# Rotary rotation in a two-layer diffusion backbone: TensorE products replaced by VectorE stream shuffles

## The reference

```python
def apply_rope(x, cos, sin):
    q = HEAD_DIM // 4
    x0, x1, x2, x3 = x[..., :q], x[..., q:2 * q], x[..., 2 * q:3 * q], x[..., 3 * q:]
    rot = jnp.concatenate([-x1, x0, -x3, x2], axis=-1)
    return x * cos + rot * sin
```

## Time and profile before

| what | us |
|---|---|
| median of 3 runs | 1592.22 |
| lowest, highest | 1591.72, 1592.33 |
| the profiled execution | 1592.69 |
| its span in the trace | 1590.7 |

### The profile page before, as it was taken

The page is one execution under the profiler, slowest core; times in us unless marked ns, Lnnn a source line. Parts: engine busy times, 40 slices in busy tenths (PEclk is TensorE's granted clock), DMA queues, the critical chain, the costliest instruction groups (busy, mean ns, idle before and its releaser), DMA issues.

```text
span 1590.7 us, 25340 instructions
## 1 busy us (share of the span) xinstructions
PE 1555.2 (98%) x10789; PEld 1291.7 (81%) x10789; DVE 785.2 (49%) x1276; ACT 550.2 (35%) x725; POOL 538.9 (34%) x243
## 2 busy tenths in 40 slices
PE   7999999899999999999999999999999999999998
PEld 3888764478888888888888888855479998998997
DVE  5898777677466633433234343666533221321224
ACT  5744335563322112221122243255544322322233
POOL 0040046313233233232323223356643444444442
PEclk9999999999999999999999999999999999999999
DMA  9532100052333333334333222200022222223223
GB/s 377 209 119 67 54 28 1 3 215 91 117 110 132 133 111 128 133 119 146 133 128 112 66 80 67 67 14 1 1 68 92 94 93 93 93 94 106 94 93 106
DMA packets 44607, 158.55 MB, mean 100 GB/s; under 512 B 4784, under 2 KB 8240, under 8 KB 42960
## 3 DMA queue, kind: packets, MB, share of 16 engines
q1 hardware_dynamic: 44064, 156.74, 28.5%
q0 software_dynamic: 432, 0.20, 0.1%
HBM read 154.95 MB, written 2.10 MB: 99 GB/s over the span
## 4 chain that ended last, share of the span: by engine, by line
PE 87%; DVE 3%; issue 1%; POOL 1%; ACT 0%; DVEq 0%; POOLq 0%
PE psum L1851 71%; PE psum L2100 3%; PE psum L2068 1%; PE psum L1999 1%; PE psum L1896 1%; PE psum L1928 1%; DVE osb L1381 1%; PE psum L2074 1%; PE psum L2072 1%; PE psum L2070 1%; PE psum L2116 1%; DVE mx L1277 1%; PE psum L1971 1%; POOL acc L622 1%; PE psum L2024 1%
## 5 line engine op out<-in xcount | busy, mean ns | idle before, releaser
L1851 PE MATMUL psum<-act,whi 128*128 128x258 f32 (+2 forms) x3968 | 784.5, 318 | 0.0
L649 POOL TENSOR_TENSOR wlo<-raw,whi 128x1024 fp32r<-128x1024 f32 (+1 forms) x162 | 391.1, 2414 | 792.1 <-ACT whi L683 792.1
L1851 PEld LDWEIGHTS psum<-act,whi 128*128 128x128 f32 x3968 | 587.8, 189 | 57.6 <-issue 3.8
L1851 PE MATMUL psum<-act,wlo 128*128 128x512 f32 (+1 forms) x1984 | 472.1, 316 | 0.0
L1851 PEld LDWEIGHTS psum<-act,wlo 128*128 128x128 f32 x1984 | 309.0, 189 | 26.8
L683 ACT ACTIVATE whi<-raw 128x1024 fp32r<-128x1024 f32 (+1 forms) x180 | 187.1, 1040 | 337.8 <-DMA raw<-weights_dram 337.8
L1178 DVE SCALAR_TENSOR_TENSOR tmps<-psum,rs 128x256 f32<-128x256 f32 (+1 forms) x176 | 78.1, 485 | 350.5 <-PE psum L1851 346.9
L1130 DVE SCALAR_TENSOR_TENSOR product<-adr,cb 128x1024 f32<-128x1024 f32 x128 | 177.5, 1418 | 6.2 <-DMA adr<-adat_dram 3.1
L1620 DVE SCALAR_TENSOR_TENSOR xT<-psum,mod,xT 128x512 f32<-128x512 f32 x93 | 58.3, 655 | 224.4 <-PE psum L1851 224.3
L1851 PE MATMUL psum<-gh,wlo 128*128 128x512 f32 x507 | 152.5, 358 | 0.0
L1851 PE MATMUL psum<-gh,whi 128*128 128x512 f32 x507 | 152.5, 357 | 0.0
(11 more groups left out here) (205 smaller groups left out, 1313.5 us busy)
## 6 DMA issues: line engine op xcount, KB each, us to landing
raw<-weights_dram SPq DMA_DIRECT2D x180, 512.0 KB, 3.5
adr<-adat_dram SPq DMA_DIRECT2D x80, 512.0 KB, 4.7
ada_w<-ada_dram SPq DMA_DIRECT2D x8, 1024.0 KB, 12.5
xT<-x_in_dram SPq DMA_DIRECT2D x3, 1024.0 KB, 16.8
xT<-x_in_dram SPq DMA_DIRECT2D x2, 1536.0 KB, 8.1
cb<-crow_dram SPq DMA_DIRECT2D x2, 1024.0 KB, 9.3
out_dram<-fin SPq DMA_DIRECT2D x8, 256.0 KB, 2.3
stage<-weights_dram SPq DMA_DIRECT2D x1, 512.0 KB, 8.1
```

The lines of the kernel that those rows point to most:

```text
L649: nc.gpsimd.tensor_tensor(wlo[:, s, 0:w], raw[:, s, 0:w], whi[:, s, 0:w].bitcast(F32), ALU.subtract).then_inc(sem("s_lo"), 1)
L1851: last = MM(out_[:, o:o + t1 - t0], w_, a_[:, t0:t1], start=k == order[0] and j == 0, stop=k == order[-1] and j == 2)
```

## The change

`rotated` is gone, with its 14 calls, the permutation matrix in the constants (128 columns) and the waits that kept its PSUM region apart from others. In its place VectorE runs a stream shuffle over the tile, ahead of the sine product: within each group of 32 partitions the halves are swapped (`SWAP`). The signs move into the table of the sine. In layer 0 the shuffle writes `ropet` in SBUF and the sine product works in place; in layer 1 it writes the PSUM bank that the product wrote. VectorE's other work and all orders stay.

```diff
 CC_BLK = CC_ONES + P
-CC_ROT = CC_BLK + P
-CC_MF = CC_ROT + P
+CC_MF = CC_BLK + P
...
+SWAP = [*range(16, 32), *range(16)]
...
         def rot_out(L, j):
 
-            if L == 1:
-                return bank(4 + j % 2)
-            return wk[(j + 1) % 2][:, 0:NX]
+            return bank(4 + j % 2) if L == 1 else ropet[0][:, 0, 0:NX]
...
             def roped_sine(L, j):
+                if L == 0:
+                    dve.wait_ge(sem("a_nrm"), j + 1)
+                    if j >= 1:
+                        dve.wait_ge(sem("a_rope"), j)
+                else:
+                    dve.wait_ge(sem("s_tile"), 19 + (j + 2 if j else 1))
+                V.stream_shuffle(rot_out(L, j), prep_tiles(L)[j][0][:, 0:NX], SWAP).then_inc(sem("a_rot"), 1)
                 dve.wait_ge(*na("rot", L, j + 1))
-                if L == 0 and j >= 1:
-                    dve.wait_ge(sem("a_rope"), j)
                 TT(ropet[L][:, j % 2 * L, 0:NX], rot_out(L, j), sin, ALU.mult).then_inc(sem("a_rsin"), 1)
...
-            def rotated(L, j):
-                if L == 0:
-                    pe.wait_ge(sem("a_nrm"), j + 1)
-                elif j >= 2:
-                    pe.wait_ge(*na("rsin", L, j - 1))
-                MM(rot_out(L, j), rot, prep_tiles(L)[j][0][:, 0:NX], start=True, stop=True) \
-                    .then_inc(sem("a_rot"), 1)
-
...
                 if n == 12:
                     pe.wait_ge(sem("g_kcpD"), 1)
                     means(1)
-                    pe.wait_ge(sem("a_rsin"), 1)
                     linear_keys(2)
                 if n == 13:
                     pe.wait_ge(sem("a_rs"), 2)
-                    rotated(0, 1)
...
                 if n == 14:
                     pe.wait_ge(sem("g_ud"), 2)
                     updates(1)
                     pe.wait_ge(sem("a_rs"), 3)
-                    rotated(0, 2)
...
-                    for m in ready_tiles(b["m"]):
-                        pe.wait_ge(sem("s_tile"), 19 + m + 1)
-                        if m == 1:
-                            values_turned(1)
-                        else:
-                            rotated(1, max(m - 1, 0))
+                    if b["m"] == 2:
+                        pe.wait_ge(sem("s_tile"), 19 + 2)
+                        values_turned(1)
...
-    con[:, CC_SIN:CC_SIN + NX] = np.tile(np.sin(ang), (2, 1))
+    con[:, CC_SIN:CC_SIN + NX] = np.tile(np.sin(ang), (2, 1)) * np.where(np.arange(P) % (2 * quarter) < quarter, -1.0, 1.0)[:, None]
```

More of the change, by code:

```diff
@@ L344, in build @@
         blk = con[:, CC_BLK:CC_BLK + P]
-        rot = con[:, CC_ROT:CC_ROT + P]
         cos = con[:, CC_COS:CC_COS + NX]
@@ L2221, in behind_block @@
                     pe.wait_ge(sem("g_kcpA"), 1)
-                    rotated(0, 0)
                 if n == 12:
@@ L2240, in behind_block @@
                     means(3)
-                    pe.wait_ge(sem("a_rsin"), 3)
                 if n == 16:
                     pe.wait_ge(sem("a_rs"), 4)
-                    rotated(0, 3)
                     pe.wait_ge(*na("mx", 0, 2))
@@ L2250, in behind_block @@
                     rows(0, 0)
-                    rotated(0, 4)
                 if pieces_within(n, 8):
@@ L2266, in within_block @@
                 if n == 14:
-                    pe.wait_ge(sem("a_rsin"), 2)
                     updates(0)
@@ L2271, in within_block @@
                     updates(2)
-                if n == 17:
-                    pe.wait_ge(sem("a_rsin"), 4)
             def gla(sums):
@@ L2394, in _shape_constants @@
     con[:, CC_BLK:CC_BLK + P] = np.kron(np.eye(2), np.ones((64, 64))) / 64.0
[L2395 to L2401, removed]
     j, i = np.arange(CH)[:, None], np.arange(CH)[None, :]
```

## The result

The changed kernel takes 1599.08 us (median of 4 runs, 1597.24 to 1601.56) beside 1591.97 for the kernel before on the same chip (4 runs). The ratio is 1.0044, interval [1.0031, 1.0056]: slower by 0.44%, 7.1 us. The profiled execution took 1600.68 us, with a span of 1597.9. Direction and range held; the size did not: 3.6 us were forecast.

What follows compares the result with a forecast made beforehand. TensorE, busy 98% of the span, was taken as the bound, with VectorE's chain pacing some blocks. Layer 0 +0.86, layer 1 +2.88 and constants -0.1 made +3.6 us, median 1592.22 to 1595.8; range 1592.0 to 1600.5.

Steps and rivals of the forecast that it cites:

- Forecast +0.86: Layer 0's five rotations together: -1.72 + 0.48 + 2.1 = +0.86 us.
- 1.72 - 0.48 = 1.24: Layer 0: first two rotations gain 1.72 us; the third makes TensorE's state updates 0.48 us later.
- 2.1: Layer 0, fourth and fifth rotations: GpSimd's weight split goes ahead of VectorE's scan, making the piece 2.1 us late.
- The rival in which GpSimd does not get in first: Layer 0: the split stays behind the scan, giving -0.4 for +0.86, total +2.4, 1594.6 us; chance 0.27.
- -1.72 was forecast: Layer 1's first two rotations, before the maxima begin: VectorE idle over 3 us, so 1.72 us gained.
- 0.68 + 0.78 + 0.68 + 1.0 = 3.14: Layer 1: delays in blocks 7, 8 and 9, then about +1.0 us at the second score step.
- s: Time from a shuffle's start to its sine product's start: 0.83 us, ends 0.61 and 1.34.
- The rival of the slow shuffle: All shuffles: the shuffle is slow, at the scan's rate; 1600.9 us; chance 0.10.
- the one in which TensorE keeps what it is given: Both layers: all fourteen removed products gained, 12 us, 1580.2 us; chance 0.09, whole or half.
- The further meeting with GpSimd: Layer 0's block 17 or layer 1's last two sums: GpSimd's turn costs another 1.3 to 2.4 us, about 1598; chance 0.14.
- Layer 1: -1.72 + 3.60 + 1.0 = +2.88 us: Layer 1's nine rotations: first two gain 1.72, blocks 5 to 9 lose 3.60, the last two triples lose about 1.0.
- 10 x 0.06: Ten shuffles counted on the path, three in layer 0 and seven in layer 1; each 0.1 us in s makes 1.0 us.

Runs made afterwards that it cites:

- e1_layer0_only: Changed kernel with shuffles in layer 0 only, layer 1's rotations again TensorE products (unsigned permutation, signed sine table); 1592.60 us, 1.0005 of the kernel before.
- e4_filler: Changed kernel with layer 1's shuffle writing SBUF, plus seven unread f32 TensorE products in layer 1; 1594.80 us, 1.0018 of the kernel before.
- e7_layer1_all: e5_reduce_first with layer 1's shuffle writing SBUF and the last two triples behind the last reduction and row tops; 1593.42 us, 1.0013 of the kernel before.
- e9_first_two: Kernel before with shuffles for the first two rotations of each layer, the other ten TensorE products (unsigned permutation, signed table); 1588.55 us, 0.9982.
- e2_layer1_only: Changed kernel with shuffles in layer 1 only, layer 0 as in the kernel before; 1598.21 us, 1.0039 of the kernel before.
- e5_reduce_first: Changed kernel with layer 1's rotary triples, from block 5 on, moved behind the next block's first reduction; 1591.46 us, 1.0001 of the kernel before.
- e11_double: Changed kernel with every shuffle done twice; 1613.87 us, 1.0143 of the kernel before.
- its control: Changed kernel with layer 1's shuffle writing SBUF, all waits kept and no added products; 1601.10 us, 1.0057 of the kernel before.

## Why the prediction was right in direction and short in size

**Layer 0, right at a constant clock.** Forecast +0.86. `e1_layer0_only`, `e4_filler` and `e7_layer1_all` have the same layer 0 and keep a granted clock of 1.00 there; counted from the products at 126 us, their piece of block 18 comes 0.74, 0.71 and 0.73 us late. By the medians, layer 0 alone costs +0.4 (-0.6 to +2.1). Each of its steps is in the trace: the updates behind the third triple wait (1.22 us at 177.16), GpSimd goes ahead of the scan, `statr` gives back a microsecond, block 18's piece is released by VectorE. In `e4_filler` the updates come 1.29 us early by the same count, where 1.72 - 0.48 = 1.24 were forecast, and from there to the piece 2.00 us are lost, where 2.1 were. The rival in which GpSimd does not get in first fell.

In the changed kernel's own profile the clock falls in layer 0 as well (0.83 between 200 and 210 us), and it costs some 0.75 us. Its row of VectorE at the end of block 17, and TensorE's two pieces in `e4_filler`:

```profile
208.40 1.02 DVE L1175 SCALAR_TENSOR_TENSOR big<-psum,rs 128x512 f32<-128x512 f32 x2 [0.79 <-PE psum L1853]
```

```profile
205.01 0.50 PE L1995 MATMUL psum<-khi,qhi 64*128 64x256 f32 x4 [1.92 <-DVE mx L1281]
...
213.48 0.50 PE L1995 MATMUL psum<-khi,qhi 64*128 64x512 f32 x2 [1.71 <-DVE mx L1281]
```

The first piece is 0.72 us earlier in the changed kernel, at 204.29, and the second at the same time, 213.47: between them VectorE waited 0.79 us for TensorE's slower products, where in `e4_filler` it waited for nothing. So the 0.98 that was read above agrees with the 0.86 by luck. It is 0.72 of the change and some 0.75 of the clock, less the 0.49 by which this execution was early.

**Layer 1's first two rotations, right.** -1.72 was forecast; the evacuation of block 4, behind both of them, begins at 995.67 and not at 996.60, 0.93 us early, which is 0.79 - 1.72. `e9_first_two` has such rotations alone, four in the two layers, and gains 3.0 us of 3.4.

**The waits of layer 1, right in kind and a little over-priced.** Block 5's piece: 0.68 forecast; from 0.93 early to 0.36 early is 0.57. Block 6's: 0.78 forecast; from 0.36 early to 0.33 late is 0.69. From there to the second score step the shift is 6.23 - 0.33 = 5.90, of which the two slow half blocks are (4.40 - 2.90) + (4.44 - 2.90) = 3.04; the 2.86 left stand against 0.68 + 0.78 + 0.68 + 1.0 = 3.14. All six waits have the releasers named. The small difference fits s, which is 0.73 us in place of 0.83; the 0.11 us that the prediction names for a slower shuffle is a difference for 2048 columns, a quarter of which would fall on 512, and the trace shows none into PSUM. The rival of the slow shuffle fell, and so did the one in which TensorE keeps what it is given. The further meeting with GpSimd came at 1019.57, where the `top` operations took 2.68 us, but TensorE had only 0.30 us of wait from it.

**The term that was missing: TensorE's clock.** The step that failed is "Layer 1: -1.72 + 3.60 + 1.0 = +2.88 us". It priced each wait at its idle time and took the products behind it to be as fast as before. They were not: 1.50 and 1.54 us in two half blocks, and 1.4 more behind the second score step (from there to the next `rows` it is 5.54 us, 1047.46 to 1053.00, and was 4.17, 1041.23 to 1045.40). Together 4.4 us. With the measured 0.79 - 1.72 + 0.57 + 0.69 + 2.86 this makes +7.6 at 1053 us (the 0.79 carries the executions' difference of about 1 us, named above); the later stages run 7.2 to 7.6 behind, and the span grew by 7.2. `e4_filler` holds VectorE's same order without the fall of the clock and stands at +2.6 us over the kernel before (interval +1.4 to +4.1); the forecast's sum with the s of a shuffle into SBUF, about 0.77, is 3.6 - 10 x 0.06 = 3.0. So the forecast priced a kernel with a constant clock rightly, and this kernel does not have one. That the measured time still lies inside the range is luck: the upper part of the range stood for a slow shuffle and a second meeting with GpSimd, and neither is what filled it.

**What stays open.** What makes the clock fall. In layer 1 of the changed kernel waits of 1.37, 1.47 and 1.47 us brought no fall and waits of 1.90, 1.72 and 2.32 did, but length does not decide it. `e2_layer1_only` kept 1.00 behind waits of 1.90 and 1.84 us and fell behind 1.72; `e5_reduce_first` kept it behind 2.01, and `e11_double` behind 2.50 in layer 0. In layer 0 the same wait of 1.92 us, behind the same work, was followed by a low clock in the changed kernel and by 1.00 in `e1_layer0_only` and `e4_filler`. The kernel before has a low stretch too (0.93 between 300 and 350 us). So each wait is a chance of a fall, not a certain one, and no run here separates what decides it.

The size moves with it from run to run. The mean granted clock of the changed kernel's four runs is 0.996, 0.996, 0.994 and 0.992, at 1597.24, 1597.48, 1600.68 and 1601.56 us. The parts of `e11_double`'s excess over ten shuffles were not taken apart one by one.

## What to carry to other kernels

When work moves off the busiest engine, price it where it arrives: an in-order engine that is half idle on average had no room in the places where a consumer waited for what stood behind the new work. If the forecast is that TensorE will wait in the middle of a busy stage, the price is the wait and, where the clock falls, the products behind it at half clock: here mostly 1.3 to 1.5 us for each fall, behind some waits of 1.7 us and more and not behind others. The better kernel was the selective one: shuffles only where VectorE had idle time in front of its next consumer (four or six of 14), which turned +7.1 us into -3.0 and -4.3.

## What was not expected of the hardware

- The granted clock fell to 0.50 inside a stage in which TensorE was over 80% busy, after some single waits of 1.7 to 2.3 us and not after others of the same length, and seven products of no use made a kernel 6.3 us faster than its control.
- Order alone can't be trusted where VectorE and GpSimd meet. A sum of 0.69 us took 2.25 to 2.89 when a GpSimd operation of 1.8 to 2.8 us began up to 0.7 us before it, and each reordering of the triple met it at a new place: mid-block splits, then the sums of the probabilities.
- A stream shuffle of 128x512 f32 is no dearer than a product: 0.69 us into PSUM, 0.73 to 0.76 into SBUF, with 14 ns for the load of its permutation.
